# Eight adaLN tiles of a two-layer diffusion step are made beside the output projection instead of beside the input projection

## What is computed

```python
def adaln(cond, w_ada, b_ada):
    m = jax.nn.silu(cond) @ w_ada + b_ada
    return jnp.split(m[:, None, :], 6, axis=-1)

sh_a, sc_a, g_a, sh_f, sc_f, g_f = adaln(c, w_ada[l], b_ada[l])
h = modulate(xs, norm_mix_g[l], sh_a, sc_a)          # rms_norm(x, g) * (1 + scale) + shift
...                                                  # z = h @ w_in, three kinds of attention, 16 heads
xs = xs + g_a * mix_out(o_mla, o_na, o_gqa, w_out[l])
xs = xs + g_f * swiglu(modulate(xs, norm_ffn_g[l], sh_f, sc_f), w_gate[l], w_up[l], w_down[l])
```

## Time and profile before

| | |
|---|---|
| median of 3 runs | 1883.92 us (1879.33 to 1889.60) |
| profiled execution | 1888.05 us, span 1886.3 us |
| busy, share of the span | PE 92%, PEld 89%, DVE 62%, ACT 37%, POOL 11% |
| mean granted TensorE clock | 0.950 |
| DMA | 159.78 MB, 85 GB/s over the span |
| layer 0: input projection | about 56 to 175 us |
| layer 0: attention | to 413 us |
| layer 0: output projection | 417 to 476 us |
| layer 0: feed-forward | to 950 us; layer 1 follows in the same order |

### The profile page before, as it was taken

One profiled execution on the slowest core, in us unless ns is written; L12 is line 12 of the kernel. 1 busy time (PEld: TensorE's weight loads), 2 busy tenths in 40 slices (PEclk: granted clock), 3 DMA queues, 4 the chain that ended last, 5 costly groups with the idle time before them and its releaser, 6 DMA issues.

```text
span 1886.3 us, 28279 instructions
## 1 busy us (share of the span) xinstructions
PE 1730.7 (92%) x11292; PEld 1677.0 (89%) x11292; DVE 1160.7 (62%) x2214; ACT 694.9 (37%) x1358; POOL 215.4 (11%) x314
## 2 busy tenths in 40 slices
PE   6888778889899999999989978899989999999997
PEld 6888767779899999999989967777889999999997
DVE  5998767863767777667462166788355445444443
ACT  2432756763422112222153365577243222112221
POOL 0001625320000000000010062533000000000001
PEclk9998799999899999999979977999989999999997
DMA  9464000032343433333122000000412222322201
GB/s 343 162 225 122 17 1 2 1 97 83 114 176 123 156 122 122 122 122 135 36 87 88 17 25 0 3 1 23 135 45 69 88 67 67 103 74 67 67 22 56
DMA packets 105397, 159.78 MB, mean 85 GB/s; under 512 B 5024, under 2 KB 83680, under 8 KB 105056
## 3 DMA queue, kind: packets, MB, share of 16 engines
q1 hardware_dynamic: 102512, 152.53, 24.1%
q0 software_dynamic: 640, 2.92, 0.6%
q10 hardware_dynamic: 2160, 3.23, 0.5%
HBM read 155.09 MB, written 3.57 MB: 84 GB/s over the span
## 4 chain that ended last, share of the span: by engine, by line
PE 76%; DVE 14%; ACT 4%; issue 3%; POOL 2%; DMA 1%; POOLq 0%; DVEq 0%; SPq 0%; ACTq 0%
PE ps L592 23%; PE ps L594 22%; PE ps L593 22%; DVE ps L1254 5%; PE ps L813 2%; PE ps L600 2%; DVE negmax L1459 2%; PE ps L792 1%; DVE K L1239 1%; PE ps L656 1%; PE ps L794 1%; DMA ada_n<-in_w_ada_first 1%; DVE hT L1239 1%; DVE pT L1239 1%; DVE Q L1350 1%
## 5 line engine op out<-in xcount | busy, mean ns | idle before, releaser
L592 PE MATMUL ps<-hT,gw 128*128 128x320 f32 x1408 | 437.1, 310 | 6.8 <-DVE hT L1239 6.8
L593 PE MATMUL ps<-hT,gw 128*128 128x320 f32 x1408 | 436.8, 310 | 0.0
L594 PE MATMUL ps<-hT,gw 128*128 128x320 f32 x1408 | 436.8, 310 | 0.0
L1318 DVE SCALAR_TENSOR_TENSOR x<-ps,mod,x 128x320 f32<-128x320 f32 (+2 forms) x576 | 211.8, 433 | 120.2 <-PE ps L594 117.1
L592 PEld LDWEIGHTS ps<-hT,gw 128*128 128x128 f32 x1408 | 266.0, 189 | 7.3 <-issue 7.3
L593 PEld LDWEIGHTS ps<-hT,gw 128*128 128x128 f32 x1408 | 265.9, 189 | 0.0
L594 PEld LDWEIGHTS ps<-hT,gw 128*128 128x128 f32 x1408 | 265.8, 189 | 0.0
L1547 DVE TENSOR_TENSOR mm<-sl,ps 128x320 f32<-128x320 f32 x88 | 42.7, 488 | 318.4 <-issue 185.3
L592 PE MATMUL ps<-act,dw 128*128 128x320 f32 x704 | 219.0, 311 | 2.7 <-DVE act L1239 2.7
L593 PE MATMUL ps<-act,dw 128*128 128x320 f32 x704 | 218.7, 311 | 0.0
L594 PE MATMUL ps<-act,dw 128*128 128x320 f32 x704 | 218.7, 311 | 0.0
(11 more groups left out here) (201 smaller groups left out, 3595.0 us busy)
## 6 DMA issues: line engine op xcount, KB each, us to landing
ada_w<-in_w_adaT SPq DMA_DIRECT2D x46, 512.0 KB, 5.9
gw_raw<-in_w_gate SPq DMA_DIRECT2D x22, 1024.0 KB, 5.5
gw_raw<-in_w_up SPq DMA_DIRECT2D x22, 1024.0 KB, 8.0
dw_raw<-in_w_down SPq DMA_DIRECT2D x22, 1024.0 KB, 4.9
ada_wf<-in_w_adaT SPq DMA_DIRECT2D x34, 512.0 KB, 7.2
wi_raw<-in_w_in SPq DMA_DIRECT2D x12, 1216.0 KB, 6.1
wo_raw<-in_w_out SPq DMA_DIRECT2D x16, 512.0 KB, 4.5
ada_wq<-in_w_adaT SPq DMA_DIRECT2D x12, 512.0 KB, 4.8
```

What stands on the lines that cost most here:

```text
L592: pe.matmul(dst, lh, rh, start=start, stop=False, skip_group_check=True)
L593: pe.matmul(dst, lh, rl, start=False, stop=False, skip_group_check=True)
L594: return pe.matmul(dst, ll, rh, start=False, stop=stop, skip_group_check=True)
L1318: i = ve.scalar_tensor_tensor(out=x[:, o, c0:c1], in0=ps[:, banks + hf_, s0:s0 + c1 - c0], scalar=mod[:, l, part * KD + o, q:q + 1], in1=x ...
```

## The change

The feed-forward's gate tiles 40 to 47 of layer 0 (`GATE`) leave the input projection. There, slices 1 to 5 carry 5, 5, 5, 5 and 4 tiles instead of 7, 7, 6, 6 and 6. The gate tiles are made in the output projection's loop on VectorE, behind the residual and the sum of squares: two each at o = 3, 4 and 5, one each at o = 6 and 7. They use a ring of 2 buffers, PSUM banks 0 and 1 for the junk products, and `silu_f`, so its SiLU moves on ScalarE from behind the second modulation to behind the split of slice 2, with a small square root behind it that brings the old table back. SP loads the first two behind cond, ahead of slice 2 of `w_out`; the loads of the others stand behind slices 4, 5 and 6, and each waits for the tile two before it. Their bias is added on VectorE behind the two low parts of `w_gate`.

```diff
+GATE = list(range(40, NADA))
+GATE_AT = [0, 0, 0, 0, 2, 4, 6, 7, 8]
+REST = list(range(ADA1, GATE[0]))
+REST_AT = [0, 0, 5, 10, 15, 20, 24]
...
+            if t >= GATE[0]:
+                return 2, t - GATE[0]
...
-                    sp.wait_ge(dots, 2 * dot_at(0, NADA - 1) + 2)
+                    sp.wait_ge(dots, 2 * dot_at(0, REST[-1]) + 2)
...
                             sp.dma_start(silu_f[:], a["cond"].unsqueeze(0).broadcast_to([P, 2, DM])).then_inc(cond_in, 16)
+                            for t in GATE[:2]:
+                                ada_load(l, t)
+                    if l == 0 and o >= 2:
+                        for t in GATE[2:][GATE_AT[o - 1]:GATE_AT[o]]:
+                            ada_load(l, t)
...
+                    if o == 2 and l + 1 < DEPTH:
+                        sc.wait_ge(cond_in, 32)
+                        sc.activation(silu_f[:], silu_f[:], ACT.Silu).then_inc(silu_done, 1)
+                        sc.activation(warm[:], eps[:], ACT.Sqrt)
...
-                if l + 1 < DEPTH:
-                    sc.wait_ge(cond_in, 32)
-                    sc.activation(silu_f[:], silu_f[:], ACT.Silu).then_inc(silu_done, 1)
...
-                        banks = ps[:, 0:2, :] if t < ADA1 else ps[:, 6:8, :]
-                        junk, after, c = banks.rearrange("p a b -> p (a b)"), own, silu_c
+                        banks = ps[:, 6:8, :] if t in REST else ps[:, 0:2, :]
+                        junk, after, c = banks.rearrange("p a b -> p (a b)"), own, silu_c if t < GATE[0] else silu_f
...
-                    ada_bias(l, ADA1, NADA)
+                    ada_bias(l, ADA1, GATE[0])
...
+                    if l == 0:
+                        if o == 3:
+                            ve.wait_ge(silu_done, 2)
+                        for t in GATE[GATE_AT[o]:GATE_AT[o + 1]]:
+                            ada(l, t)
...
+                if l == 0:
+                    ve.wait_ge(dots, 2 * dot_at(0, NADA - 1) + 2)
+                    ve.tensor_tensor(mod[:, 0, GATE[0]:NADA, :], mod[:, 0, GATE[0]:NADA, :],
+                                     b_ada[:, 0, GATE[0]:NADA].unsqueeze(2).broadcast_to([P, KD, 2]), ALU.add)
...
-                if l + 1 < DEPTH:
-                    ve.wait_ge(silu_done, 2)
```

More of the change, by code:

```diff
@@ L53 @@
 FIRST = list(range(BY_PE, ADA1))
-REST = list(range(ADA1, NADA))
-REST_AT = [0, 0, 7, 14, 20, 26, 32]
+GATE = list(range(40, NADA))
+GATE_AT = [0, 0, 0, 0, 2, 4, 6, 7, 8]
+REST = list(range(ADA1, GATE[0]))
+REST_AT = [0, 0, 5, 10, 15, 20, 24]
 AHEAD = [list(range(NADA * b // (FB - 1), NADA * (b + 1) // (FB - 1))) for b in range(FB - 1)] + [[]]
```

## The result

| | median us (lowest to highest, runs) | profiled execution: us, span, granted clock |
|---|---|---|
| before, same comparison | 1878.64 (1873.80 to 1889.73, 13) | 1888.05, 1886.3, 0.950 |
| after | 1866.97 (1862.28 to 1877.45, 13) | 1874.98, 1873.2, 0.957 |

The ratio is 0.9939, 95% interval 0.9917 to 0.9960: 0.61% or some 11.5 us faster (7.5 to 15.6). The forecast was 10.1 us. Most of that is the base: the sum was taken off the median of the three runs then shown (1883.92), and thirteen runs of the same kernel, those three among them, have theirs at 1878.64.

A forecast was written before the change was run, and what follows sets the result against it. VectorE was taken to bound layer 0's input projection, TensorE the output projection. -15.1 us there and +5.0 us here (4.5 plus 0.5) gave -10.1 us, so 1873.8 us from the median 1883.92; range 1868 to 1881.

The forecast's parts named there:

- part 1: Layer 0's input projection: eight tiles fewer on VectorE, TensorE never waits; 14.8 us plus 0.3 at K's copy, sum -15.1 us.
- part 1 gives less: Input projection rival: a late tile or slice load leaves 10 to 13 us gained, net -5 to -8; chance 0.10.
- everything up to the end of attention would come 15 us earlier: Sign of being right: from the input projection's last evacuation to attention's end all stays the same, 15 us earlier.
- Part 2: Output projection loads: two tile loads ahead of the third `w_out` slice delay it; cost 0.5 us, bounds 0 to 1.5.
- a wait for `wo` that ends on a DMA: Output projection, sign of being wrong: TensorE's wait for a `w_out` slice goes back to a load; no size given.
- the margins of 1, 1 and 0 us: Output projection: slack forecast for `w_out` slices 5, 6 and 7, queued behind tile loads on SP; cost 0.
- Part 3: ScalarE, output projection: SiLU and two table loads after the third split take 4.7 us; cost 0, margin 1.5 us.
- Part 4: Output projection: VectorE's two-tile rounds take 8.4 us against TensorE's 7.04, stalling it; with the longer end, +4.5 us.
- the tail: Output projection after output 6: VectorE is busy until 39.8, output 7's residual starts 0.8 us late, token sums at 41.7.
- The clock at the new stalls: Output projection rival: TensorE's clock falls at the new stalls, net -6 to -8, 1876 to 1878 us; chance 0.18.
- The range: Whole kernel: 1868 to 1881 us, taking in -4 to -13 us and the differences between medians of three runs.
- A feed-forward that changed: Feed-forward, sign of being wrong: this stage would differ from the kernel before; no size given.

The follow-up runs named there:

- the last version with six tiles: Against the changed kernel: six gate tiles moved, first two loads behind slice 2, others one slice later, low part between tiles; 1869.03 us (0.9921), again 1867.64 us (0.9912).

## Why the prediction was right, and where it was off

The mechanism came out as forecast, and the difference as closely as the time can tell; the time itself lies outside the stated range. The step that failed is the base from which the sum was taken, the median of 1883.92 us, which accounts for 5.3 of the 7 us.

**What bounds, and part 1: right.** The restarts are gone, 80.16 us is reached exactly, and the K copy brings the 0.3 us: -14.82 - 0.33 = -15.15 us by the marks, forecast -15.1. The ready times of the slices were forecast at 90.5, 106.6, 122.7 and 140.1; the low parts ended at 90.4, 106.4, 122.4 and 139.6. The last evacuation was at 159.90, forecast 159.7. The rival *part 1 gives less* fell. That everything up to the end of attention would come 15 us earlier did not hold in this profile: the first split of `w_out` came 10.5 us earlier, and 14.7 and 17.3 in the other two profiles of the change, by the spread of attention.

**Part 2, the slice behind two tile loads: mechanism right, size within its bounds.** The wait for slice 2 was to be 0.5 us, at most 1.5. It was 2.22, 1.90 and 0.21 in three profiles of the change. The sum took both TensorE's start and the slice's arrival as fixed, and both vary. In the kernel before, TensorE was at the lower of its two levels at first and the first output took 426.89 - 416.88 = 10.0 us. In the change the clock was 0.72 over those microseconds and it took 415.17 - 406.34 = 8.8; in the third profile of the change it was slow again, and took 10.0, and there the slice also came 0.8 us sooner (15.97 against 16.77 us behind the first matmul). The two slow starts (kernel before, then the third profile of the change):

```profile
416.00:422.00 6.00, 5.12 (x19) 5.15 (x20) 1.87 (x2) 0.42 (x1) 0.00 (x0) 0.50 1.09 368
```

```profile
399.50:405.00 5.50, 5.38 (x20) 5.42 (x21) 1.10 (x1) 0.00 (x0) 0.00 (x0) 0.50 1.09 366
```

So TensorE waits more where it was quicker just before, and the wait's length is not its price. From the first matmul to output 2 it is 24.09 us before, and 25.39, 25.59 and 24.59 in the three profiles of the change: a cost of 1.3, 1.5 and 0.5 us, where 0.5 was said. The prediction also named a wait for `wo` that ends on a DMA as a sign of being wrong, beside its own 0.5 us for just such a wait; the sign did come, with slice 2 alone. Slices 5 to 7 cost nothing, as forecast; the margins of 1, 1 and 0 us came out at 1.3 and 1.6 on VectorE for slices 5 and 6, and at 0.5 on TensorE for slice 7, with 1.18 us of waiting on VectorE.

**Part 3, SiLU: right.** Two table loads and SiLU took 427.72 - 423.09 = 4.6 us, forecast 4.7, and slice 3's low part was ready at 430.0 (begun at 428.80), before TensorE asked. The Trainium skill (ScalarE: Activation LUTs, What ACT_TABLE_LOAD costs) has a drain of 1.38 us with every switch; here SiLU starts 0.01 us after the table load ends (423.09 + 1.28 = 424.37, and 424.38), and the next load starts 0.02 us after SiLU (424.38 + 1.92 = 426.30, and 426.32). By the rule TensorE would have waited for slice 3; it did not, in any of the profiles.

**Part 4, VectorE's rounds: the mechanism right, the sum 1.3 us too high.** Two terms were mis-sized. A round was put at 8.4 us and is 8.10: two tiles in a row take 5.18, not 2 x 2.69, since the small accumulator read of the second starts together with the next instruction (both at 446.06), and the low part takes 1.14 for 1.22. By TensorE's starts (431.52, 439.24, 447.34, 455.44, 462.58, against 7.04 each) the stalls cost 0.7, 1.1 and 1.1 us and 0.1 behind them, 2.9 in all, where 0.8, 1.4, 1.4 and 0.15 were added up to 3.8. The second is the tail. VectorE needs 470.13 - 462.78 = 7.35 us from output 6's residual to output 7's, where 7.8 was summed, so output 7's residual starts 0.3 us late and not 0.8: 470.13 - 431.73 = 38.40 us behind output 2, before 35.20, and 2.9 of the 3.2 are the stalls. The token sums follow 1.91 us later, against 1.93 before. From output 2 to the token sums it became 40.31, before 37.13: +3.2 where +4.5 was said, and below the 41 to 43 us that were to show it.

**Net.** By the stages -15.15 + 1.30 + 3.18 = -10.7 us, with part 2 as in the third profile -11.5; forecast -10.1, measured -11.5 with 4 us to either side. The stage from the first split to the root says 70.57 - 66.10 = +4.5 in this profile, +6.7 and +3.7 in the other two, forecast +5.0. These sums leave out the feed-forward, which took 2.9 to 3.4 us less in all three profiles of the change (below), and attention, which varies by more than that. With the feed-forward the stages of the first pair give -13.6. All of this lies in the measured interval of 7.5 to 15.6, so that -10.1 and -11.5 are so close is in part luck: the stages of the two projections confirm the sum, the time does not resolve it.

**The clock at the new stalls: this rival fell.** In the three profiles of the change, waits of 0.2 to 2.2 us for slices 2, 4, 5 and 6 were never followed by a lower clock; the first matmul took 0.41 or 0.42 us each time. The Trainium skill (TensorE: Matmul & The Clock Gate, A second HAM failure mode: psum-queue depth-cycling) tells of a bf16 kernel in which short idles between groups of matmuls bring the lower clock about; the short idles of this stage did not, in any profile of the change.

**The range: the step that failed.** The 1868 to 1881 was laid around 1883.92 us, the median of three runs, with a few us allowed for it; that base was 5.3 us above the median of thirteen. The difference was right to 1.4 us and the absolute time wrong by 7. Off 1878.64 the same sum gives 1868.5 us, 1.6 above the result. More runs alone would not have fixed the base: in the three later comparisons the same kernel had medians of 1878.05 (nine runs), 1879.95 and 1883.65 us (eleven each), and beside the last the change had 1869.13, inside the range. The change's ratio was 0.9939, 0.9930 and 0.9930. Why the base moves from one comparison to the next stays open.

**A feed-forward that changed**, which the prediction named as a sign of being wrong, did come: 463.0 for 465.9 us. The cause is one wait in its first block that is the same in both kernels. In the kernel before, and with the clock of the microseconds around it:

```profile
522.51 0.63 PE L592 MATMUL ps<-act,dw 128*128 128x320 f32 x1 [2.65 <-DVE act L1239]
```

```profile
520.00:525.00 5.00, 2.49 (x9) 2.49 (x10) 4.41 (x8) 2.76 (x4) 0.00 (x0) 0.68 0.98 396
525.00:530.00 5.00, 5.00 (x25) 5.00 (x24) 3.90 (x11) 0.00 (x0) 0.00 (x0) 0.63 0.60 192
```

And in the changed kernel:

```profile
516.34 0.41 PE L601 MATMUL ps<-act,dw 128*128 128x320 f32 x1 [2.65 <-DVE act L1249]
```

```profile
514.00:519.00 5.00, 2.66 (x18) 2.66 (x19) 4.41 (x8) 2.77 (x4) 0.00 (x0) 1.00 0.95 382
```

From this matmul to the end of the feed-forward it is 423.9 us in all three profiles of the kernel before and 421.1 in all three of the change. The same wait of 2.65 us was followed by the lower level in the first three and in none of the others. Of its variants, four have the short feed-forward (462.7 to 463.0 us), two lie between (464.5 and 465.0), and the last version with six tiles has either (465.97 and 462.97). It is worth 2.9 us where it falls out well. Whether the change makes it likelier, or 3 against 3 is chance, stays open.

## What to carry to other kernels

Work on an engine that bounds one stage moves well into a stage that another engine bounds, and both sides can be counted from the trace before: what comes out is limited by the next engine (15.1 of 21.5 us here), and what goes in costs a round's excess over the bound's period. The loads decide as much as the work: a load that must wait for its buffer holds up every load behind it in the same queue, so it goes behind those that are needed sooner; the order alone made 23 us here, lower clock included, and moving the consumer earlier than its load made things worse. And a forecast in absolute time has to allow for the base: here medians of nine to thirteen runs of one kernel lay between 1878 and 1884 us, while the ratio of the two kernels in one comparison moved by 0.1%.

## What was not expected of the hardware

The times follow the granted clock. The thirteen runs of the change were 1862.3 and 1862.4 us at 0.965 and 0.967, 1865 to 1867 at 0.960 to 0.962, two of 1870 at 0.956 and 0.960, and 1875 to 1877 at 0.955 to 0.957, with the same instructions. In the profiles it is above all attention, where TensorE stops often, that takes 237.3 to 247.0 us in the same code: 237.7 us at 0.94, 244.0 at 0.91 and 247.0 at 0.88 in layer 0.

The token sums after the output projection took 1.28 us for the first ten matmuls in one profile of the change and 2.30 in another, after the same wait of 2.26 us:

```profile
468.10 2.30 PE L609 MATMUL ps<-ones,rstd 128*128 128x2 f32 x10 [2.26 <-DVE rstd L1289]
```

That is 2.0 of the 2.3 us by which this profile's stage (72.83) is longer than the first: from the token sums to the root it is 4.47 us against 2.43. So after waits of 2.0 to 3.0 us TensorE went on at the full clock in one place or profile and not in the other. The 2.99 us of the earlier trace rows were followed by a first matmul of 0.41 us, and a wait of 2.98 us for the same slice in the third profile of the kernel before by one of 0.62. In the projections and the feed-forward the first matmul took 0.42 us at most after every wait of 0.2 to 2.3 us, and 0.57 or more after every wait above 3.0, in all fourteen profiles. Why one execution goes on at full clock and the next not, and with it most of the spread of the times, no run here settles.
